# Gathering an expert's U and V row with one 8 KB indirect DMA for blocks 1 to 3 of a product-key expert layer

## What is computed

```
s = einsum('thcd,hckd->thck', q, sub_keys)
top_s, top_i = top_k(s, 16)
cand_s = top_s[:, :, 0, :, None] + top_s[:, :, 1, None, :]
best_s, pos = top_k(cand_s, 16)
gate = softmax(best_s)
u = take(expert_u, ic)
h = gelu(einsum('cd,ced->ce', xc, u))
vv = take(expert_v, ic)
out = einsum('ce,ced->cd', gc * h, vv)
x = layer_norm(ALPHA * x + out)
```

## Time and profile before

| | before |
|---|---|
| median of 3 runs | 1891.44 us (1889.11 to 1896.01) |
| the profiled execution: span from first to last instruction | 1889.7 us (no other time of it is given) |
| instructions | 14555 |
| PE, DVE, POOL, ACT busy | 67%, 68%, 57%, 13% |
| transfers | 603.28 MB, 319 GB/s over the span |
| of them gathered rows | 536.94 MB in 1024 indirect DMAs |
| granted TensorE clock, mean | 0.820 of 2.4 GHz |

### The profile page before, as it was taken

How to read it: one execution, slowest core, us unless ns; L and a number is a source line. 1 busy time by engine, 2 the same in 40 slices (tenths; PEclk the granted TensorE clock), 3 DMA queues, 4 the chain that set the end, 5 groups by cost and what they waited for, 6 DMA issues and landing times.

```text
span 1889.7 us, 14555 instructions
## 1 busy us (share of the span) xinstructions
PE 1258.4 (67%) x3056; PEld 582.3 (31%) x3056; DVE 1289.4 (68%) x2842; ACT 238.6 (13%) x570; POOL 1073.2 (57%) x1253
## 2 busy tenths in 40 slices
PE   6778979563789776456666565665656565566665
PEld 3565446231346432122222221222222222222221
DVE  1348988789668866666767676767576667666556
ACT  0110000112111111011100111100101011111110
POOL 0004344335446667657767666667676767667774
PEclk9889989676989888777777878777877887778787
DMA  7668787857589889889999998899999999899996
GB/s 267 239 245 321 300 316 278 295 181 277 212 284 386 296 311 365 313 313 355 360 348 356 345 363 308 322 352 349 361 349 344 348 369 335 323 345 358 350 369 262
DMA packets 180946, 603.28 MB, mean 319 GB/s; under 512 B 18720, under 2 KB 21024, under 8 KB 180768
## 3 DMA queue, kind: packets, MB, share of 16 engines
q0 software_dynamic: 147456, 536.94, 77.2%
q1 hardware_dynamic: 33440, 65.80, 9.6%
HBM read 600.57 MB, written 2.10 MB: 319 GB/s over the span
## 4 chain that ended last, share of the span: by engine, by line
PE 24%; issue 20%; DVE 18%; DMA 17%; POOL 15%; another core or an unknown queue 1%; ACT 1%; POOLq 1%; DVEq 0%; SPq 0%; ACTq 0%
POOL ring L376 14%; DMA ring<-peer_v,stage 10%; PE ACC L428 9%; DVE ring L953 6%; PE W L483 6%; DMA ring<-peer_u,stage 6%; PE W L489 2%; PE W L659 2%; PE X L631 2%; DMA wt<-w_in 1%; PE ACC L631 1%; PE W L631 1%; DVE best_i L1207 1%; DVE xs L1001 1%
## 5 line engine op out<-in xcount | busy, mean ns | idle before, releaser
L428 PE MATMUL ACC<-ring,diag 128*128 128x512 f32 x1272 | 783.5, 774 | 476.6 <-DMA ring<-peer_v,stage 442.1
L953 DVE SCALAR_TENSOR_TENSOR ring<-ring,X 128x1024 f32<-128x1024 f32 x512 | 613.3, 1219 | 316.0 <-DMA ring<-peer_u,stage 288.1
L376 POOL DMA_INDIRECT ring<-peer_u,stage x512 | 522.1, 1020 | 410.1 <-DVE ring L953 214.1
L376 POOL DMA_INDIRECT ring<-peer_v,stage x512 | 503.0, 982 | 246.0 <-issue 153.8
L428 PEld LDWEIGHTS ACC<-ring,diag 128*128 128x128 f32 x1272 | 298.5, 248 | 956.7 <-issue 889.8
L771 ACT ACTIVATE diag<-ident,gate 128x128 f32<-128x128 f32 x318 | 122.8, 399 | 895.3 <-PE ACC L428 627.2
L1001 DVE SCALAR_TENSOR_TENSOR xs<-ring,gate,xs 128x1024 f32<-128x1024 f32 x96 | 123.3, 1284 | 53.6 <-DMA ring<-peer_v,stage 45.0
L483 PE MATMUL W<-wt,actT 128*128 128x512 f32 x320 | 143.9, 607 | 12.6 <-DMA ident<-ident_in 11.5
L659 PE MATMUL W<-actT,wt 128*128 128x128 f32 (+1 forms) x512 | 116.4, 389 | 1.4 <-ACT actT L833 1.4
L973 DVE SCALAR_TENSOR_TENSOR xs<-ring,gate,xs 128x512 f32<-128x512 f32 x98 | 73.3, 748 | 47.8 <-DMA ring<-peer_v,stage 45.7
L659 PEld LDWEIGHTS W<-actT,wt 128*128 128x128 f32 x512 | 80.1, 198 | 36.7 <-issue 2.7
(11 more groups left out here) (180 smaller groups left out, 804.3 us busy)
## 6 DMA issues: line engine op xcount, KB each, us to landing
wt<-w_in SPq DMA_DIRECT2D x14, 2048.0 KB
wt<-peer_w_query SPq DMA_DIRECT2D x8, 2048.0 KB
wt<-w_out SPq DMA_DIRECT2D x4, 2048.0 KB
ring<-peer_u,stage POOLq DMA_INDIRECT x512
ring<-peer_v,stage POOLq DMA_INDIRECT x512
out<-xs SPq DMA_DIRECT2D x4, 512.0 KB, 5.4
actT<-xT SPq DMA_DIRECT2D x1, 1536.0 KB, 11.7
xs<-x SPq DMA_DIRECT2D x1, 1536.0 KB, 14.1
```

Source lines behind the costliest of these rows:

```text
L376: pool.indirect_dma_start(out=ring[:, r, :], out_offset=None, in_=table, in_offset=bass.IndirectOffsetOnAxis(ap=stage[:, half, c:c + 1], a ...
L428: last = nc.tensor.matmul(ACC[:, half * HW:(half + 1) * HW], diag[:, odd, m, :], ring[:, r, half * HW:(half + 1) * HW], start=start and m ...
L953: STT(out=ring[:, r, :], in0=ring[:, r, :], scalar=1.0, in1=X[:], op0=ALU.mult, op1=ALU.mult, accum_out=hid[:, bass.ds(e, 1)]).then_inc(sl ...
```

## The change

1. The host joins the two tables into one, `uv`, of 16384 rows x 2048 floats (8 KB).
2. Block 0 is fetched as before from that table, by its halves (`rows` has 32768 rows of 4 KB; block 0's indices are doubled, and V is reached by an element offset). All its 16 V groups are now fetched before anything else (before: 11, and 40 rows mixed in). Of groups 11 to 15 slots 3, 5, 7 go to PE and five slots to DVE.
3. Blocks 1 to 3: one indirect DMA per expert slot brings 128 rows of 8 KB (1.05 MB), 384 in all, straight from `idx`, without the copies. They go to 18 slots (NS) of 2048 floats per partition, laid over the buffers of the mixer (`arena`): slots 0 to 5 are free when the mixer is done, 6 to 13 when the last key scores are (EARLY), 14 to 17 are the old ring (LATE).
4. DVE makes the dots only (`pair_dot`). For each four experts (FG) ACT does gelu, DVE multiplies with the gates (`weigh`), ACT makes four diagonals (`fdiag`, six buffers, ND), PE sums all V halves (`add_pairs`). The sum of a block alternates between `ACC` and `ACC2`, the token between `X` and `X2`, in the banks of `W`.
5. The retrievals stand between groups of four as before between mixed groups, always a quarter or two ahead; the residual's factor is applied in `join_sums`.

The diff, cut to its core:

```diff
+V_GROUPS = E // RING
+ALONE = 11
+NF = (NB - 1) * E
+NS = 18
+EARLY, LATE = 6, 14
+FG = 4
+ND = 6
...
-        ring = sb("ring", [P, RING, D])
+        arena = sb("arena", [P, NS * 2 * D])
+        fused = [arena[:, i * 2 * D:(i + 1) * 2 * D] for i in range(NS)]
...
             for i in range(V_GROUPS):
                 n = AT_V + i
-                one_table(peer_v, i * RING, n, n % 2, n)
-            with pool.Fori(0, MIXED // PERIOD) as quarter:
-                pool.wait_ge(experts_ready, quarter + 5)
-                for j in range(PERIOD):
-                    both_tables(quarter * QUARTER + (E + j * HALF), quarter * QUARTER + (E - LAG + j * HALF),
-                                quarter * PERIOD + (AT_MIXED + j), (AT_MIXED + j) % 2,
-                                quarter * (2 * PERIOD) + (AT_MIXED + 2 * j))
-            for i in range(TAIL):
...
+                one_table(D, i * RING, n, n % 2)
+            for n in range(NF):
+                slot = n % NS
+                if n % QUARTER == 0:
+                    pool.wait_ge(experts_ready, 4 + n // QUARTER + 1)
+                if n == 0:
+                    pool.wait_ge(mixer_ready, 2 * NB)
+                elif n == EARLY:
+                    pool.wait_ge(keys_scored, 4 + 3 * WQ)
+                elif LATE <= n < NS:
+                    for r in (2 * (n - LATE), 2 * (n - LATE) + 1):
+                        pool.wait_ge(slot_used[r], AT_V + V_GROUPS + 1)
+                elif n >= NS:
+                    pool.wait_ge(pairs_summed, n - NS + 1)
+                pool.indirect_dma_start(
+                    out=fused[slot], out_offset=None, in_=uv,
+                    in_offset=bass.IndirectOffsetOnAxis(ap=idx[:, E + n:E + n + 1], axis=0),
+                ).then_inc(pair_landed[slot], 16)
...
+            def add_pairs(b):
+
+                if b > 1:
+                    pe.wait_ge(sum_read, b - 1)
+                for n in range((b - 1) * E, b * E):
+                    first, last_one = n % E == 0, n % E == E - 1
+                    pe.wait_ge(pair_diag_ready, n + 1)
+                    for half in range(2):
+                        last = nc.tensor.matmul(
+                            sum_of(b)[:, half * HW:(half + 1) * HW], fdiag[:, n % ND, :],
+                            fused[n % NS][:, D + half * HW:D + (half + 1) * HW], start=first, stop=last_one)
+                    last.then_inc(pairs_summed, 1)
...
+            def pair_group(g):
+
+                cols = slice(E + g * FG, E + (g + 1) * FG)
+                act.wait_ge(pair_dotted, (g + 1) * FG)
+                nc.scalar.activation(hid[:, cols], hid[:, cols], ACT.Gelu).then_inc(pair_gelu_ready, 1)
+                act.wait_ge(pair_weighed, g + 1)
+                for n in range(g * FG, (g + 1) * FG):
+                    if n == 0:
+                        act.wait_ge(slot_used[PE_SLOTS[-1]], AT_V + V_GROUPS + 1)
+                    elif n >= ND:
+                        act.wait_ge(pairs_summed, n - ND + 1)
+                    nc.scalar.activation(fdiag[:, n % ND, :], ident[:], ACT.Copy,
+                                         scale=gate[:, E + n:E + n + 1]).then_inc(pair_diag_ready, 1)
...
+            retrieve(1, 1)
+            gate_norm(4)
+            gate_norm(5)
+            for g in range(NF // FG):
+                for n in range(g * FG, (g + 1) * FG):
+                    if n % E == 0:
+                        dve.wait_ge(token_in_psum, n // E + 2)
+                    pair_dot(n)
+                    if g and n % FG == 0:
+                        weigh(g - 1)
+                q = g // 8 + 6
+                if q < 4 * NB:
+                    if g % 8 == 1:
+                        best_keys(*divmod(q, 4))
+                    elif g % 8 == 3:
+                        best_pairs()
+                    elif g % 8 == 5:
+                        best_experts(*divmod(q, 4))
+                    elif g % 8 == 7:
+                        gate_norm(q)
...
```

More of the change, by code:

```diff
@@ L242, in build @@
         row_landed = [sem(f"row_landed{i}") for i in range(RING)]
+        pair_landed = [sem(f"pair_landed{i}") for i in range(NS)]
         stored = sem("stored")
@@ L371, in _, with one_table @@
                 nc.gpsimd.sem_inc(slot_used[r], 1)
[L372 to L383, removed]
+            rows = uv.rearrange("e (c d) -> (e c) d", c=2)
+            def one_table(at, first, n, half):
                 nc.gpsimd.tensor_copy(stage[:, half, :], idx[:, bass.ds(first, RING)]).then_inc(staged, 1)
-                pool.wait_ge(staged, staged_before + 1)
+                pool.wait_ge(staged, n + 1)
                 for r in range(RING):
[L388 to L396, removed]
+                    pool.wait_ge(slot_used[r], n + 1)
+                    nc.gpsimd.sem_inc(staged_tick, 1)
+                    pool.indirect_dma_start(
+                        out=ring[:, r, :], out_offset=None, in_=rows,
+                        in_offset=bass.IndirectOffsetOnAxis(ap=stage[:, half, r:r + 1], axis=0),
+                        element_offset=at,
+                    ).then_inc(row_landed[r], 16)
             per = QUARTER // RING
@@ L704, in _ @@
             query(1, WAVES[1])
-            for b in range(NB):
-                add_block(b)
+            beside(range(2 * ALONE + sum(BESIDE_QUERY), 2 * V_GROUPS))
+            for b in range(1, NB):
+                add_pairs(b)
         @block.scalar
@@ L1006, in tail, with pair_dot @@
-            def tail(lo, hi):
-                for i in range(lo, hi):
-                    n = AT_TAIL + i
-                    for m, r in enumerate(DVE_SLOTS):
-                        last = DVE_SLOTS[m - 1] if m or i else DVE_SLOT
-                        added = sum(len(dve_slots(g)) for g in range(V_GROUPS)) + i * len(DVE_SLOTS) + m
-                        add_halves(NB - 1, r, n, NB * E - LAG + i * RING + r, added, last, n + 2 if m else n + 1)
+            def pair_dot(n):
+                b = 1 + n // E
+                slot = n % NS
+                dve.wait_ge(pair_landed[slot], 16 * (n // NS + 1))
+                STT(out=fused[slot][:, 0:D], in0=fused[slot][:, 0:D], scalar=1.0, in1=token_of(b), op0=ALU.mult,
+                    op1=ALU.mult, accum_out=hid[:, E + n:E + n + 1]).then_inc(pair_dotted, 1)
```

253 lines of the change are left out of this document (102 added, 151 removed).

## The result

The changed kernel takes 1701.01 us (median of 4 runs, 1698.70 to 1702.15); the kernel before took 1890.28 beside it (4 runs). The ratio is 0.8994, 95% interval 0.8976 to 0.9012: 10% faster. The profiled execution took 1698.70 us with a span of 1696.9.

A forecast was written before the change was run, and what follows sets the result against it. POOL's issue pace and late slots were taken to keep the transfer queue from being full. Front 708.6 + transfers 1009 + end 22.8 + 0.8 gave a span of 1741.2, so 1743 us, range 1705 to 1828.

The forecast's parts named there:

- What bounds, and what unbinds it: Mixed groups: POOL's issues and late slots hold transfers at 342 GB/s; fewer, larger DMAs and 18 slots fill the queue.
- Until 703 us: Front with block 0: nearly unchanged, fifth group's end at 703.23 us, last ring row landing at about 708.6, retrievals +0.8 us.
- POOL: Issue of 384 fused DMAs: 1.245 us each whatever the bytes, 478 us, so POOL leaves the path.
- the doubled price: POOL's issue in the fused loop: an 8 KB row costing twice a 4 KB one, 956 us or 1014.
- The transfers: Fused stretch of blocks 1 to 3: 402.65 MB at 399 GB/s, 1009 us, 2.63 us per expert.
- the four best stretches of before: Kernel before, four 20 us stretches with all slots in flight: 397, 404, 390 and 404 GB/s, share just over 1.
- My low end, 1705: Bottom of the forecast range: a queue a little better than any stretch shown, 410 to 415 GB/s, 1705 to 1715 us.
- The end: Behind the last landing: dot, gelu and weights, diagonal, four PE rows at 8.7, then join, norm and store: 22.8 us.
- PE, DVE, ACT: Engine work in the fused stretch, all hidden: DVE some 740 of 1009 us, ACT at most 218, PE costed at nothing.
- The first (357 GB/s kept): Fused stretch: memory, not issue, limits over long stretches; 1128 us of transfers, 1862 in all; chance 0.08.
- The second: Fused stretch: PE becomes the bound in part at 2.83 us per row, 1087 for 1009, 1821 in all; chance 0.08.
- the third: Fused stretch: PE at 1.2 GHz throughout, 3.75 us per row, 2180 us in all, slower than before; chance 0.04.

The follow-up runs named there:

- Experiment 1: Changed kernel with each expert of blocks 1 to 3 fetched by two DMAs of 4 KB rows, 18 slots kept: 1842.45 us, ratio 0.9709 to the kernel before.
- experiment 4: Changed kernel with fewer slots than 18: 14 slots 1703.30 us, 10 slots 1758.58 us, 7 slots 2245.05 us.
- experiment 5: Changed kernel with one V row in four of blocks 1 to 3 added on DVE again: 1702.96 us, ratio 0.8972 to the kernel before.
- POOL's relief alone: Kernel before, its mixed groups reading indices without POOL's two copies and the wait behind them: 1863.19 us, ratio 0.9875.
- experiments 3: Changed kernel with every second expert fetched as two 4 KB rows: 1715.07 us, ratio 0.9071 to the kernel before.
- 7: Changed kernel with early fused rows, block 1's first retrieval cut, smaller last groups: 1704.53 us; second try, second retrieval spread over three groups: 1694.80 us.
- experiment 6: Kernel before with parts of the change: all V sums of mixed groups on PE 1879.76 us; no index copies on POOL 1863.19; both 1866.33.

## Why the prediction was right and wrong

*What bounds, and what unbinds it*: right. POOL's issues and the slots kept the queue part empty, the long transfers with 18 slots fill it. Experiment 1 shows that the slots are not enough without POOL's margin, experiment 4 that the margin alone doesn't keep the queue full with 7 or 10 slots and does with 14; experiment 5 that the sums on PE are not where the gain lies. Of the slots six or seven were held, where I had nine.

*Until 703 us*: right. The first fused row was issued at 700.77 us (forecast 703.2). Counted back from the end of most transfers, 1664.4 less 955.3 (402.65 MB at 421.5 GB/s), the fused transfers run full from 709.1; forecast 708.6.

*POOL*: right. 0.94 us per DMA whatever the row's bytes; the doubled price is out.

*The transfers*: **this is the step that failed.** The term was 402.65 MB at 399 GB/s, 1009 us; it measured 421.5 GB/s, 955 us. I had taken the mean of the four best stretches of before for the full rate, and carried a rate of 4 KB rows to 8 KB rows; two of the four stretches held transfers of weights beside the rows. The runs split the 54 us in two: a full queue of 4 KB rows gives 410 (982 us, 27 less), and 8 KB rows 422 (27 less again). I had argued myself that a share of 0.95 is not a full queue, and then took 1.01 to 1.03 for one. My low end, 1705, stood for 410 to 415 GB/s, "a little better than any stretch shown": it had no allowance for the larger row at all, though the change makes exactly that.

*What I did not have*: the engine that is behind the others at the end, 11.6 us (1664.4 to 1676.04), which gave back a part of those 54.

*The end*: 20.9 us against 22.8; the last four rows took PE 7.13 us, near the lower bound of 7.1, where I took 8.7.

*PE, DVE, ACT*: PE needed (502.5 + 253.0) / 384 = 1.97 us per row, at a granted clock of 0.82 to 0.92; hidden. Four rows are 7.9 of the 10.0 us that their transfers take; I had 10.3 of 10.5, so there was more room than I thought, though a transfer takes 2.49 and not 2.63. The end of my argument, that PE's pause goes and the clock is 1.00 then, was not put to the test: the pauses stayed. DVE's dots came to 464 us and 31 for reading the sums out, 495 of the 500 costed, and the diagonals to 0.39 each.

The sum with what was measured: 709.1 + 955.3 + 11.6 + 20.9 = 1696.9, the span. It closes by construction, since 709.1 is counted back from 1664.4; what it shows is where the time lies.

*Rivals.* The first (357 GB/s kept) is out: 421 GB/s held for 950 us. The second and the third are out by 1.97 us per row; they needed 2.83 and 3.75.

The rule that I weighed, the Trainium skill's 358 GB/s (DMA: Bandwidth & Descriptors, section Bandwidth), is not this case's limit. The same section of the Trainium skill marks its measured 425 GB/s for 16 MB as a figure for one core with its pair idle, and the Trainium skill's HBM Reference, section Specifications (TRN2), says that a core alone is held by its 16 DMA engines at about 425 GB/s. Runs here agree: 422 for 8 KB rows. By that figure the term would have been an estimated 947 us; I had read one sentence and not its neighbour.

## What to carry to other kernels

Take the full rate from a stretch in which nothing can hold the queue (many transfers issued ahead), for the size of row that the new code uses; a transfer share near 1 is no proof of a full rate. When a time lands where a theory put it, look in the trace for the theory's mechanism too: with 10 slots and with POOL's relief alone the number was right and the mechanism another. When gathers bound a kernel, look at how far the issuing engine is ahead: it needs clearly fewer microseconds per transfer than the transfer itself (1.24 for 2.49 here; 2.49 for 2.56 was not enough), and enough slots to cover the longest stretch in which nobody frees one. The slots without the margin gave 2.9% here, the margin with 10 slots 7.4%, both 10%. Once the queue is full, only its start, its dry spots and what stands behind the last landing are worth work.

## What was not expected of the hardware

- The rate is that of the single engines. Between 1665 and 1676 us, by the share of 0.07, one engine of 16 was at work, and an expert's sixteenth, 65.5 KB, took 2.46 us: 26.6 GB/s, and 16 such make 426. In the full stream it was 421.5 / 16 = 26.3. Alone it was hardly faster than in company.
- That one engine was behind is open in its cause. In the run with transfers alone, whose stretches are 160 to 240 us long, all ended within 2 us. From 700 to 1665 us the changed kernel's trace has 33 packets of instruction code with 0.37 MB on two queues; at 26.6 GB/s on one engine they would take 13.9 us, near the 11.6. That they all fall to that engine was not shown. The other runs narrow it down. From the half rate to the last transfer it is 9.5 to 11 us in the six whose queue stayed full almost throughout (the changed kernel and experiments 3, 5, 7 and, with 14 slots, 4; 31 to 34 packets). With the same 33 packets it is 3.0 us with 10 slots, and 0.5 us in experiment 1 with 36: this fits a late engine that catches up wherever the queue runs dry, and speaks against a lag that goes by the packets alone. The Trainium skill (DMA: Bandwidth & Descriptors, section Latency and other measured facts) tells of two engines that are usually slower; which one it was here no view shows.
- In some whole kernels POOL has pauses of up to 6 us that the trace puts down to "remote": 97 us in experiment 1, and 51, 35 and 70 in the three runs of experiment 6. The traces of the kernel before and of the changed kernel show none, nor does the run without computation. Their cause is open; in the run with POOL's relief alone they are 35 of the 56 us that came back.
